# A mixture-of-experts layer that streams its weights: a ring of eight 2 MB slots in place of six and three single-use regions, with 4 MB loads for the gate/up weights

## The reference, cut to what matters

```python
logits = xt @ w_router + b_router
top_val, top_idx = lax.top_k(logits, 4)
gates = softmax(top_val)
# for each expert e, for the tokens that chose it:
h = xb @ w_gate_up[e] + b_gate_up[e]         # [rows, 1024] @ [1024, 2048]
g, u = h[:, :1024], h[:, 1024:]
g = minimum(g, 7.0); u = clip(u, -7.0, 7.0)
y = ((u + 1) * g * sigmoid(1.702 * g)) @ w_down[e] + b_down[e]   # [rows, 1024] @ [1024, 1024]
# out = sum over a token's 4 experts of gate * y, then x = layer_norm(alpha * x + out)
```

## Time and profile before

| | |
|---|---|
| median of 3 runs | 1233.39 us (1231.67 to 1236.79) |
| the profiled execution | 1232.36 us, of which its span (first to last instruction) 1230.5 us |
| TensorE busy, mean granted clock | 1153.1 us (94%), 0.996 |
| VectorE, ScalarE, GpSimd busy | 219.0, 133.9, 48.6 us |
| DMA | 445.50 MB in 54,349 packets, mean 362 GB/s |
| the chain that ended last, by engine | PE 50%, DMA 46%, DVE 2% |
| gate/up and down loads | 125 into the ring and 3 early, and 64, each 2048 KB |
| late loads of ScalarE | 512 KB, 512 KB, 128 KB |

### The profile page before, as it was taken

One profiled execution on the slowest core, in us unless ns is written; L12 is line 12 of the kernel. 1 busy time (PEld: TensorE's weight loads), 2 busy tenths in 40 slices (PEclk: granted clock), 3 DMA queues, 4 the chain that ended last, 5 costly groups with the idle time before them and its releaser, 6 DMA issues.

```text
span 1230.5 us, 13113 instructions
## 1 busy us (share of the span) xinstructions
PE 1153.1 (94%) x5364; PEld 523.2 (43%) x5364; DVE 219.0 (18%) x550; ACT 133.9 (11%) x288; POOL 48.6 (4%) x59
## 2 busy tenths in 40 slices
PE   7999999999999999989899999998989898999985
PEld 5686746854334343423243434333333333332421
DVE  1133112114211111111112112111111111111113
ACT  2033101211000000000000001000000000000002
POOL 0023103210000000000000000000000000000000
PEclk9999999999999999999999999999999999999998
DMA  9934243367899999999999999999999999999994
GB/s 355 314 135 156 81 159 137 137 248 297 339 378 427 428 429 429 428 427 430 428 428 429 427 426 428 429 428 428 429 428 429 428 430 428 428 429 428 429 427 183
DMA packets 54349, 445.50 MB, mean 362 GB/s; under 512 B 10120, under 2 KB 11280, under 8 KB 29744
## 3 DMA queue, kind: packets, MB, share of 16 engines
q1 hardware_dynamic: 52160, 440.48, 86.2%
q10 hardware_dynamic: 2160, 4.60, 1.1%
HBM read 444.01 MB, written 1.06 MB: 362 GB/s over the span
## 4 chain that ended last, share of the span: by engine, by line
PE 50%; DMA 46%; DVE 2%; issue 1%; ACT 1%; SPq 0%; POOL 0%; DVEq 0%
DMA ring<-in_w_gate_up 45%; PE bank L1490 18%; PE bank L1172 9%; PE bank L1185 9%; PE bank L1513 6%; PE bank L1397 2%; PE bank L1473 1%; PE bank L1458 1%; PE bank L1342 1%; PE bank L1500 1%; PE bank L1144 0%; PE bank L1245 0%; PE bank L1320 0%; DMA x_nat<-in_x 0%; PE bank L1258 0%
## 5 line engine op out<-in xcount | busy, mean ns | idle before, releaser
L1490 PE MATMUL bank<-ring,PT 128*64 128x512 f32 x2000 | 444.4, 595 | 43.0 <-DMA ring<-in_w_gate_up 43.0
L1490 PEld LDWEIGHTS bank<-ring,PT 128*64 128x64 f32 x2000 | 139.7, 137 | 341.6 <-issue 256.6
L1513 PE MATMUL bank<-ring,NCt 128*64 128x512 f32 x1024 | 227.2, 596 | 0.7 <-ACT NCt L712 0.7
L1513 PEld LDWEIGHTS bank<-ring,NCt 128*64 128x64 f32 x1024 | 70.8, 137 | 153.3 <-issue 141.1
L1172 PE MATMUL bank<-reg_bc,ring 128*128 128x256 f32 x512 | 113.7, 381 | 1.8 <-ACT reg_bc L637 1.8
L1070 DVE TENSOR_SCALAR reg_k<-bank 128x512 f32<-128x512 f32 x32 | 22.1, 691 | 469.6 <-PE bank L1490 469.6
L1172 PEld LDWEIGHTS bank<-reg_bc,ring 128*128 128x128 f32 x512 | 96.4, 190 | 18.0 <-issue 5.4
L703 ACT ACTIVATE reg_v<-reg_k 128x512 f32<-128x512 f32 x32 | 20.2, 630 | 748.2 <-DVE reg_k L1070 748.2
L1087 DVE COPY reg_v<-bank 128x512 f32<-128x512 f32 x32 | 22.1, 691 | 303.9 <-PE bank L1513 303.9
L1397 PEld LDWEIGHTS bank<-L,reg_a 128*128 128x128 f32 x512 | 62.9, 196 | 24.8 <-issue 23.5
L1397 PE MATMUL bank<-L,reg_a 128*128 128x128 f32 x512 | 69.3, 288 | 1.0 <-DVE L L984 0.7
(11 more groups left out here) (203 smaller groups left out, 497.5 us busy)
## 6 DMA issues: line engine op xcount, KB each, us to landing
ring<-in_w_gate_up SPq DMA_DIRECT2D x125, 2048.0 KB, 24.6
ring<-in_w_down SPq DMA_DIRECT2D x64, 2048.0 KB, 20.4
ring<-in_w_in SPq DMA_DIRECT2D x6, 2048.0 KB, 15.1
ring<-in_w_ck SPq DMA_DIRECT2D x2, 2048.0 KB, 20.2
ring<-in_w_cv SPq DMA_DIRECT2D x2, 2048.0 KB, 9.8
ring<-in_w_mix_out SPq DMA_DIRECT2D x2, 2048.0 KB, 7.6
ring<-in_w_cq SPq DMA_DIRECT2D x2, 2048.0 KB, 7.7
ring<-in_w_co SPq DMA_DIRECT2D x2, 2048.0 KB, 9.5
```

Of the source, the lines that this page charges most:

```text
L1490: last = mm(ps[half * CAP:(half + 1) * CAP, :], xgT[:, k, i * CAP:(i + 1) * CAP], w[:, j, col:col + HALF], start=False, stop=(k == KD - 1) ...
L1513: last = mm(xy_ps[half * CAP:(half + 1) * CAP, :], hT[:, a:a + CAP], w[:, j, half * HALF:(half + 1) * HALF], start=(k == 0), stop=(k == KD ...
```

## The change

- The ring has eight slots of 2 MB for the whole layer. `reg_q` and `reg_bc` are now slots 6 and 7; `reg_kv` holds no weights any more, its first 512 columns hold the SwiGLU result (`hbuf`). Before the experts start, eight pieces are loaded in place of nine. The buffers take the same memory.
- Gate/up weights are laid out with four rows for each partition (32 KB from consecutive addresses) and come in two loads of 4 MB an expert. Each fills two neighbouring slots, and waits until both are free. Experts 0, the second part of 1, and 31 still come in 2 MB halves with 16 KB packets. Down weights: two loads of 2 MB as before.
- Experts 2 to 11 and 28 to 31 are loaded as soon as their slots are free (`load_expert`). For experts 12 to 27 and further blocks (`load_later`) each load waits for the piece of its kind of the expert before, as with six slots.
- The slots repeat after four experts, so TensorE's loops hold two pairs, and the blocks for experts with over 64 tokens come in fours.
- `x2` and the SwiGLU result are stored in the order in which the stationary operands take them: `gather` and `transpose_h` read columns without stride. The operations that write them (ScalarE's `normalise`, GpSimd's gain and bias, VectorE's `gain2`, `scale_and_bias2` and line 1078) write with 128 values between neighbours, and `base` reads `x2` so as the moving operand.

```diff
-CH = 6
-GUC = 4
-GUJ = KD // GUC
-DNJ = KD // (CH - GUC)
-SLOT = GUJ * 2 * F
+GUJ = 4
+DNJ = 4
+SLOT = 4096
+NSLOT = 8
+PERIOD = 4
+LEAD = 12
...
-        ring = sb("ring", [P, CH, SLOT])
+        ring = sb("ring", [P, NSLOT, SLOT])
...
-        reg_bc = sb("reg_bc", [P, 2, KD, T])
+        reg_bc = ring[:, 7, :].rearrange("p (r k t) -> p r k t", r=2, k=KD)
...
-        reg_q = sb("reg_q", [P, 4096])
+        reg_q = ring[:, 6, :]
...
+        def x2_half(tt, half):
+            return x2[:, tt, half * HALF:(half + 1) * HALF].rearrange("p (j q) -> p q j", j=GUJ)
...
+        def slot_of(e, chunk):
+
+            return (6 * e + chunk) % NSLOT
...
+        def gate_up_slots(e, c):
+            at = slot_of(e, 2 * c)
+            return ring[:, at:at + 2, :].rearrange("p a (j n) -> p (a j) n", j=2)
...
+            def load_expert(e, n, r, halves=False):
+
+                sp.wait_ge(gate_up_in[0], n * 16)
+                if halves:
+                    sp.wait_ge(chunks_used, n * 4 - 4)
+                    load_half(e, 0, 0)
+                sp.wait_ge(y_done, n - 1)
+                if halves:
+                    load_half(e, 0, 1)
+                    sp.wait_ge(chunks_used, n * 4 - 3)
+                    load_half(e, 1, 0)
                 else:
...
+                    load_gate_up(e, 0, r)
+                sp.wait_ge(gate_up_in[1], n * 16)
+                sp.wait_ge(chunks_used, n * 4 - 2)
+                if halves:
+                    load_half(e, 1, 1)
                 else:
...
+                    load_gate_up(e, 1, r)
+                sp.wait_ge(down_in[0], n * 16)
+                sp.wait_ge(chunks_used, n * 4 - 1)
+                load_down(e, 0, r)
+                sp.wait_ge(down_in[1], n * 16)
+                sp.wait_ge(gu_done, n)
+                load_down(e, 1, r)
+
+            def load_later(e, n, r):
+
+                sp.wait_ge(chunks_used, n * 4 - 2)
+                load_gate_up(e, 0, r)
+                sp.wait_ge(gu_done, n)
+                load_gate_up(e, 1, r)
+                sp.wait_ge(chunks_used, n * 4)
+                load_down(e, 0, r)
+                sp.wait_ge(y_done, n)
+                load_down(e, 1, r)
...
-                nc.vector.scalar_tensor_tensor(out=x2[:, 1, cols], in0=x1[:, 1, cols], scalar=mv[:, 1, 1, 0:1],
-                                               in1=lng[1][:, cols], op0=ALU.subtract, op1=ALU.mult).then_inc(gained2_dve, 1)
+                nc.vector.scalar_tensor_tensor(out=x2_half(1, half), in0=by_rows(x1[:, 1, cols]), scalar=mv[:, 1, 1, 0:1],
+                                               in1=by_rows(lng[1][:, cols]), op0=ALU.subtract, op1=ALU.mult).then_inc(gained2_dve, 1)
...
-                    nc.vector.scalar_tensor_tensor(out=ubuf, in0=ubuf, scalar=1.0, in1=gbuf,
+                    nc.vector.scalar_tensor_tensor(out=hbuf.rearrange("p (j q) -> p q j", j=DNJ), in0=by_rows(ubuf), scalar=1.0,
+                                                   in1=by_rows(gbuf),
                                                    op0=ALU.add, op1=ALU.mult).then_inc(h_ready, 1)
...
-                        mm(acc[tt][half][:, :], K[:, C_AID:C_AID + P], x2[:, tt, half * HALF:(half + 1) * HALF],
+                        mm(acc[tt][half][:, :], K[:, C_AID:C_AID + P], x2_half(tt, half),
```

More of the change, by code:

```diff
@@ L455, in _ @@
[L455 to L471, removed]
-                else:
[L473 to L478, removed]
@@ L480, in _, with load_half @@
-            sp.wait_ge(tables_ready, 1)
[L481 to L487, removed]
+            def load_half(e, c, half):
+                done = (gate_up_half_in, gate_up_in)[half][c]
+                sp.dma_start(two_rows(e, c, half), gate_up_source(e, c, HALVES[half])).then_inc(done, 16)
@@ new lines, in load_later @@
+            def load_later(e, n, r):
[7 more added lines that the diff above has]
+                load_down(e, 1, r)
+            for e in range(2, LEAD):
+                load_expert(e, e, e % PERIOD)
+            with sp.Fori(LEAD // PERIOD, NE // PERIOD - 1) as q:
+                for r in range(PERIOD):
+                    load_later(q * PERIOD + r, q * PERIOD + r, r)
@@ new lines, in _ @@
+            for e in range(NE - PERIOD, NE):
+                load_expert(e, e, e % PERIOD, halves=e == NE - 1)
+            sp.wait_ge(tables_ready, 1)
+            rounds = sp.value_load(ctl[0:1, MAXX:MAXX + 1], min_val=0, max_val=MAXX // PERIOD)
+            with sp.If(rounds > 0):
+                with sp.Fori(0, rounds) as q:
+                    for r in range(PERIOD):
+                        e = sp.value_load(ctl[0:1, bass.ds(q * PERIOD + r, 1)], min_val=0, max_val=NE - 1)
+                        load_later(e, q * PERIOD + (r + NE), r)
@@ L1483, in gate_up @@
                     c, j = k // GUJ, k % GUJ
-                    if j == 0:
-                        pe.wait_ge(chunk_in[c], n * 16 + 16)
-                    w = chunk_tile(c, i if first else None)
+                    if halves[c] and j == 0:
+                        pe.wait_ge(gate_up_half_in[c], halves[c] * 16)
+                    elif j == (2 if halves[c] else 0):
+                        pe.wait_ge(gate_up_in[c], n * 16 + 16)
+                    w = gate_up_row(k, r)
                     for ps, c0 in ((gate_ps, 0), (up_ps, F)):
@@ L1518, in down, with pair @@
                     last.then_inc(y_done, 1)
-            def pair(p, first=False, with_base=False, last=False):
-                gate_up(p, 0, first)
+            def pair(p, r, first=False, with_base=False, last=False):
+                gate_up(p, 0, r, (1, 1) if first else (0, 0))
                 if not first:
@@ L1539, in pair @@
                 pe.wait_ge(hT_sb, p * 2 + 1)
-                down(p, 0, range(KD), first)
-                gate_up(p, 1, first)
+                down(p, 0, r)
+                gate_up(p, 1, r + 1, (0, 2) if first else (2, 3) if last else (0, 0))
                 if not last:
@@ L1555, in pair @@
                 pe.wait_ge(hT_sb, p * 2 + 2)
-                down(p, 1, range(KD), first)
+                down(p, 1, r + 1)
             wait_evacuated(pe, ("rT", 0, 1))
```

153 lines of the change are left out of this document (92 added, 61 removed).

## The result

The changed kernel took 1235.96 us (median of 20 runs, 1234.0 to 1240.04) beside 1232.16 us (1231.34 to 1237.02) for the kernel before: ratio 1.0026, 95% interval 1.0017 to 1.0034. It is slower by 3 to 4 us, within the 0.5% that the forecast called no change, but 10.5 us above the predicted 1225.5 and outside its range. Of the two gains foreseen, the larger packets are there; five losses took them back.

What follows compares the result with a forecast made beforehand. The DMA engines, full at 428 GB/s in steady state, were taken as the bound, TensorE close behind. Terms 4.2 + 4.2 - 0.5 = 7.9 us gave 1225.5 us beside the median; range 1222 to 1231, the likeliest case 1223 to 1228.

Steps and rivals of the forecast that it cites:

- the two gains foreseen: Lasting eighth slot with an earlier full load queue, 4.2 us, and 32 KB packets, 4.2 us.
- Step 1: Load queue at expert 2: lasting eighth slot lands the 17th piece at 351.2, not 355.45, ScalarE's loads costing 2.9; gain 4.2 us.
- restart: After expert 0's down matmuls, at 321.4, expert 2's first 4 MB load restarts the queue, landing at 333.7.
- step 4: Writers on VectorE at 512 bytes' distance: 0.15 us more each, restart and end 0.5 us later (bounds -0.2 and +1.8).
- Step 2: 4 MB gate/up loads: 32 KB packets save 75 ns a load, 4.2 us over 56 loads (bounds 0 and some 6).
- B: Gate/up loads: 32 KB rows move no faster than two of 16 KB; 1229.7 us; chance 0.22.
- D: 4 MB loads: larger loads are slower; at 420 GB/s it costs 15.5 us, time 1241; chance 0.08.
- Step 3: TensorE's gathers without stride: 110 ns a pass instead of 130, worth 0.2 us before expert 0, otherwise cover for waits.
- the tail: End of the kernel behind the last gate/up piece, TensorE and normalisation: 28.3 us, 1202.2 to 1230.5.
- Step 5: 4 MB pieces, six slots' distance from expert 12: 1.3 us margin at the routing tables, doubled base would cost 2.1; taken as 0.
- rival C: Routing tables at expert 12: the load queue runs dry, costing 2.1 us, time 1227.6; chance 0.08.
- Rival E: TensorE's granted clock: longer waits lower it, over 4.6 us lost each pair makes TensorE the bound, above 1233 us; chance 0.02.

Runs made afterwards that it cites:

- the sixth: The change with eight slots' distance for all experts, 32 KB packets, tokens stored in pairs, SwiGLU result in natural order: 1230.38 us, 0.9978 of the kernel before.
- the fifth: The change with eight slots' distance, 4 MB loads in 16 KB packets, tokens at a stride of two, SwiGLU result in natural order: 1234.35 us, 1.0009.
- the fourth: The change with only the SwiGLU result put back in natural order, tokens left as changed: 1236.92 us, 1.0037 of the kernel before.
- the ninth: The kernel before with TensorE's loops of one pair written as loops of two pairs, nothing else: 1236.89 us, 1.0028 of the kernel before.
- tenth: The sixth with experts 12 to 27 issued at six slots' distance, as in the change: 1232.51 us, 0.9992 of the kernel before.
- eleventh: The fifth with each 2 MB gate/up piece a load and a wait of its own: 1232.88 us, 0.9992 of the kernel before.
- The first experiment: The change with eight slots' distance for every expert, no later wait for experts 12 to 27: 1233.17 us, 0.9999 of the kernel before.

## Why the prediction was wrong, by its steps

The sum forecast a span of 1222.6; it was 1236.0, so 13.4 us are to be found.

**Step 1, slot and restart.** The mechanism is right: in the 16 KB kernel the 17th piece landed at 351.4 instead of 355.45, 4.0 of the 4.2. Two terms were mis-sized. ScalarE's loads cost 5.1 instead of 2.9: 2.2. I had divided their bytes by a rate between the two of the earlier trace rows, but 1.18 MB in small packets among large ones took more than their bytes. And the restart was 2.1 later, not the 0.5 of step 4: 1.6.

**Step 2, packets.** Right: 29.2 us a period, and the sixth beside the fifth; rivals B and D fall. The ceiling and slope fitted by two sizes held for the third.

**Step 3, no stride.** The value was about nil, as taken, but the statement on the rule was wrong. I compared the gather's 130 ns with the 110 of other transposes; the same gather without stride takes 124. The two-hit rule of the Trainium skill (SBUF — State Buffer, Specifications (TRN2), Cachelines) does agree with the gathers: a stride of 8 bytes, with two values a line, costs 5%; one of 16 bytes, with one value a line, doubles the pass (246). The transposes at 16 bytes, 207 ns a weight load instead of 144, show a smaller price. Had I held the change's base passes against the rule, I would have feared a doubling there, which the runs then showed (6.97 against 3.44).

**Step 4, writers.** Mis-sized: 0.36 us an operation (692 to 1051), near the upper bound of 0.4, not 0.15. Most of the restart's delay is something else, the granted clock of 0.61 in expert 0's SwiGLU: 1.6 us by the chain (0.89 on L1538, 0.75 on L1580, by the rows of other experts). It was taken as excluded from a window at 1.00 in the kernel before. Its trigger is open: with VectorE's time restored in the fourth, expert 1 still started at 323.04, and the ninth, the old data layout with the new loop, shows 0.93 there too; but in the fifth, sixth, tenth and eleventh, with the same loop, expert 1 started at 321.4 to 321.9. TensorE's pause before these passes does not decide it either: 2.76 us in the change, 2.42 in the ninth and 2.42 in the kernel before, where the clock held. The step also said that the write of the SwiGLU result is hidden later. In expert 31 it is not: no load covers it, and its 0.35 us more is in the tail below.

**Step 5, six slots' distance.** This is the largest failure. The base passes doubled, rival C's condition, which I gave 0.08 and a price of 2.1. My margin was 1.3 us; the base used 3.5, with the clock (8.78 at 613.4) and VectorE's 0.36 on top. In the chain the same point of an expert, its third and fourth pieces, lies at 613.40 in expert 11 and at 794.96 in expert 17: 181.6 us where six periods of 29.21 are 175.3, so 6.3 lost. Of it 3.9 is the stop before the landing at 680.5. The pairs' kernels have 611.35 and 788.21 (eight slots) and 611.13 and 787.97 (six): 176.9 and 176.8, so 1.6 is lost in this stretch without any gap, and the gap proper is 4.7, more than twice rival C's price of 2.1. The first experiment regained 3.9 of span, and the tenth, with the base at 3.46, had no gap.

**Not in the forecast.** Late landings, by the ninth experiment probably those of instruction fetches: one of 1.5 us near the end (30.77 against 29.2), and probably the 1.6 just named. TensorE's loops had grown with the change, and no term stood for that. The tail: with waits gone after 1176.45, TensorE ended the last expert at a clock of 0.74 (8.81 us instead of 7.11 for the down passes), and with VectorE's 0.35 the tail behind expert 31's last piece was 2.0 us more than 28.3. My step 5 kept loads last.

Together: 1.6 + 2.2 + 6.3 + 1.5 + 2.0 = 13.6, against 13.4. The terms are read from one execution each, and the change's was 1237.82 us long, 1.9 above the median, so the close sum is partly luck. Rival E, the clock, was right in kind (it fell eight times) and wrong in price: TensorE did not become the bound of the middle, but lost time at the two places without cover.

## What to carry to other kernels

A change of layout moves a stride from one reader to several others: list every operation that touches the tensor, and price each by a run of that operation. When a margin is 1 us, a cost of unknown size beside it is the forecast, not a detail: here undoing either of two costs kept the queue full. And the number of instructions in a loop's body is itself a change; the 1.0028 of the unrolled kernel is as large as the net effect of the whole change, 1.0026.

## What the runs showed of the hardware that was not expected

- A packet of 32 KB costs about 9 ns less than two of 16 KB: period 29.20 against 29.34 us, with the same bytes.
- Strides in 32-bit words: a gather's pass, stationary of 128 by 128, 124 ns without, 130 at 8 bytes, 246 at 16 bytes; but four transposes of that size 0.63 us without and 0.72 at 16 bytes. Moving operand of 512 values at 512 bytes' distance: 3.44 to 6.97 us for eight. VectorE's write at 512 bytes: 692 to 1051 ns.
- 1.18 MB of small loads in a full queue held the large ones up by 5.1 us.
- Ten more packets of instruction fetch, 16 KB each, went with 4.6 us of span, 3.0 of it as two late landings of a saturated stream.
- TensorE's granted clock fell in short stretches (0.63 from 613.4 to 618) behind five of ten waits of 2.6 us for weights; 613.40 shows 8.78 us instead of 7.1 for 32 passes. In the 16 KB kernels it fell behind seven of ten waits of 2.7 us or more, and with waits of at most 1.3 us it stayed up until the last expert.
